# The short sequences' delta rule, moved from behind the prompt's head pairs to between their steps

## The reference

```python
q = _l2norm(q) * dk ** -0.5; k = _l2norm(k)
gc = jnp.cumsum(g, axis=-1)
decay = where(incl, exp(gc[..., :, None] - gc[..., None, :]), 0)
m = where(strict, einsum('bhnid,bhnjd->bhnij', kb, k) * decay, 0)
u, w = triangular_solve(eye + m, [v * beta, kb * exp(gc)])
# per chunk:
v_new = u_n - w_n @ s
o_n = qd_n @ s + qk_n @ v_new
s = s * gt_n + kd_n.T @ v_new
```

## Time and profile before

| what | value |
|---|---|
| median of the runs | 3092.52 us |
| the profiled execution itself | 3093.57 us |
| span of its instructions | 3091.7 us |
| PE busy | 2939.6 us (95%) |
| DVE / ACT / POOL busy | 45% / 29% / 9% |
| DMA | 225.42 MB, mean 73 GB/s |
| mean granted clock of TensorE | 0.947 |

### The profile page before, as it was taken

The page is one execution under the profiler, slowest core; times in us unless marked ns, Lnnn a source line. Parts: engine busy times, 40 slices in busy tenths (PEclk is TensorE's granted clock), DMA queues, the critical chain, the costliest instruction groups (busy, mean ns, idle before and its releaser), DMA issues.

```text
span 3091.7 us, 50936 instructions
## 1 busy us (share of the span) xinstructions
PE 2939.6 (95%) x21018; PEld 2804.5 (91%) x21018; DVE 1378.2 (45%) x1701; ACT 895.8 (29%) x1253; POOL 275.2 (9%) x307
## 2 busy tenths in 40 slices
PE   7999999998898889999999999999999999999997
PEld 6999999987887589999999999999967789999997
DVE  4434357735643354343464443434543434333355
ACT  3222234433221132221233232222344423222232
POOL 4000012202230230000010000000100000000011
PEclk9999999998897589999999999999988889999998
DMA  4222222220002213222222332322211212222221
GB/s 117 76 81 82 82 82 82 82 67 1 3 2 57 68 41 88 87 83 82 72 78 80 127 85 81 87 85 72 94 57 65 81 55 82 82 82 82 78 85 44
DMA packets 306823, 225.42 MB, mean 73 GB/s; under 512 B 8014, under 2 KB 300287, under 8 KB 306687
## 3 DMA queue, kind: packets, MB, share of 16 engines
q1 hardware_dynamic: 306674, 224.30, 24.1%
q0 software_dynamic: 64, 0.00, 0.0%
HBM read 212.14 MB, written 12.13 MB: 73 GB/s over the span
## 4 chain that ended last, share of the span: by engine, by line
PE 91%; DVE 4%; issue 1%; ACT 1%; POOL 1%; DMA 1%; another core or an unknown queue 0%; DVEq 0%; SPq 0%; POOLq 0%; ACTq 0%
PE ps L448 73%; PE ps L1005 2%; PE ps L1018 1%; PE ps L1472 1%; PE ps L1512 1%; PE ps L1015 1%; PE ps L1514 1%; PE ps L1451 1%; PE ps L1479 1%; PE ps L1085 1%; PE ps L1519 1%; PE ps L1097 1%; PE ps L1060 1%; PE ps L1441 1%; DVE w_lo L424 1%
## 5 line engine op out<-in xcount | busy, mean ns | idle before, releaser
L448 PE MATMUL ps<-hx_hi,w_hi 128*128 128x320 f32 (+1 forms) x3986 | 860.7, 297 | 13.0 <-DVE hx_lo L1585 8.5
L448 PE MATMUL ps<-hx_lo,w_hi 128*128 128x320 f32 (+1 forms) x3986 | 860.5, 296 | 0.0
L448 PE MATMUL ps<-hx_hi,w_lo 128*128 128x320 f32 (+1 forms) x3986 | 846.1, 293 | 0.0
L414 ACT ACTIVATE w_hi<-raw 128x1024 fp32r<-128x1024 f32 (+2 forms) x378 | 382.0, 1012 | 1317.4 <-PE ps L448 1300.2
L448 PEld LDWEIGHTS ps<-hx_hi,w_hi 128*128 128x128 f32 x3986 | 606.1, 188 | 15.7 <-issue 7.0
L448 PEld LDWEIGHTS ps<-hx_lo,w_hi 128*128 128x128 f32 x3986 | 617.2, 190 | 0.0
L448 PEld LDWEIGHTS ps<-hx_hi,w_lo 128*128 128x128 f32 x3986 | 610.3, 188 | 0.0
L424 DVE TENSOR_TENSOR w_lo<-raw,w_hi 128x1024 fp32r<-128x1024 f32 (+2 forms) x378 | 470.4, 1245 | 120.8 <-ACT w_hi L414 120.5
L448 PE MATMUL ps<-hid_hi,w_hi 128*128 128x320 f32 (+1 forms) x1664 | 358.5, 297 | 11.1 <-DVE of L910 8.3
L448 PE MATMUL ps<-hid_lo,w_hi 128*128 128x320 f32 (+1 forms) x1664 | 357.4, 296 | 0.0
L448 PE MATMUL ps<-hid_hi,w_lo 128*128 128x320 f32 (+1 forms) x1664 | 356.2, 295 | 0.0
(11 more groups left out here) (364 smaller groups left out, 2558.7 us busy)
## 6 DMA issues: line engine op xcount, KB each, us to landing
raw<-in_ffn_w_in SPq DMA_DIRECT2D x176, 512.0 KB, 5.0
raw<-in_ffn_w_out SPq DMA_DIRECT2D x64, 512.0 KB, 4.3
raw<-in_a_w_in SPq DMA_DIRECT2D x33, 512.0 KB, 4.1
raw<-in_ffn_w_out SPq DMA_DIRECT2D x32, 384.0 KB, 3.4
raw<-in_ple_w_gate SPq DMA_DIRECT2D x16, 512.0 KB, 4.1
raw<-in_w_kv SPq DMA_DIRECT2D x16, 512.0 KB, 4.0
k_page<-in_cache_k SPq DMA_DIRECT2D x16, 512.0 KB, 4.1
v_page<-in_cache_v SPq DMA_DIRECT2D x16, 512.0 KB, 4.4
```

The source lines that it names most:

```text
L414: nc.scalar.activation(w_hi[:, m, 0:k], s.view(m, slot), ACT.Copy).then_inc(w_hi_done, 1)
L448: last = nc.tensor.matmul(TILE[m][:, c0:c1], w[:, m, k], h[:, k, c0:c1], start=k == 0 and a == 0, stop=k == k_all - 1 and a == 2)
```

## The change

- The loop over the pairs is written out four times (`for hp in range(NG)`), so that other steps can stand between those of one pair.
- A lane has three banks instead of four (`lane_bank(a, j)` is bank `3 * a + j`). Banks 6 and 7 belong to the sample steps (`S_BANK`). With a bank less, the broadcast of beta into a lane comes after `qn` has read bank 0, and the transposes of `v` come after `mt` has read bank 1, for both lanes, behind the products.
- The sample steps stand between those of the pairs. In the table (pair, level) is in the inverse, between `am` and `dm` on PE; (pair, i2) is behind chunk 2 of the recurrence.

| pair 0 | pair 1 | pair 2 | pair 3 |
|---|---|---|---|
| level 2 `bc` of q, k | level 1 `am1` | set-up `su4` | set-up `su2` |
| level 3 `bc` of g, beta | level 2 `dm1`, `dtm1` | level 2 read 1 | level 2 `su6` |
| level 4 `kk`, `qk` | level 3 `am2` | level 3 `vtr1` | level 3 read 3 |
| level 5 `vt` | level 4 `dtm2` | level 4 `om1` | level 4 `vtr3` |
| level 6 `kt` | level 5 `wm`, `ut` | level 5 `su1` | level 5 `om3` |
| i2 `xtr` | level 6 read 0 | level 6 `su5` | level 6 `su3` |
| | i0 `vtr0`, i1 `om0`, i3 `su0` | i0 read 2, i1 `vtr2`, i2 `om2` | i0 `su7`, i1 to i3 sums of squares |

- The read, the new rows and the output are made for two heads at a time (q and q + 4, "group q"). DVE, ACT and POOL have their sample steps behind both lanes of a level in the same way, so that what DVE makes in one level PE takes in the next.
- The states of group q are loaded when pair q has used its keys and values, whose place they take.
- The sample tensors move to the place of `w_hi`, `w_lo` and `raw`. The `ab` product therefore prepares no unit of `a_w_out`; `gdn_sp` loads its two first units behind `su7`, and ACT and DVE split unit 0 behind the squares.
- The squares of heads 0 to 5 are made on POOL, those of 6 and 7 on ACT; the sums for heads 0 to 5 stand in the recurrence of pair 3.
- PE takes the row that it spreads from `e32_r`, made once, instead of `sel`, which POOL made for each pair.

```diff
-        following = {id(s): f for s, f in zip(products, products[1:] + [None])}
+        following = {id(s): None if s.kind == "ab" else f for s, f in zip(products, products[1:] + [None])}
@@ the places of the sample tensors
-        r = Region(scratch0, hx1)
-        vnm = [r.at]
+        r = Region(split0, split1)
+        S_BANK = (6, 7)
+        def lane_bank(a, j):
+            return bank(3 * a + j)
+        SUMS = ps[:, 6:8, 0:HC]
@@ gdn_pe
-            with pe.Fori(0, HA // 2) as hp:
+            for hp in range(NG):
...
+                for a in range(2):
+                    h = 2 * hp + a
+                    pe.wait_ge(g["qn"], h + 1)
+                    pick = e32_r[64:64 + HA, h:h + 1].to_broadcast((HA, P))
+                    mm(lane_bank(a, 0), pick, rows_hi[64:64 + HA], start=True, stop=False)
+                    mm(lane_bank(a, 0), pick, rows_lo[64:64 + HA], start=False, stop=True).then_inc(g["bcb"], 1)
+                if hp == 2:
+                    sample_update(0, 4)
+                if hp == 3:
+                    sample_update(2, 2)
...
+                    if (hp, level) == (0, 2):
+                        sample_norms()
...
+            def sample_norms():
+                after(pe, "mq_s", "mk_s", "mg_s", "mb_s")
+                spread(bank_a, dx_s, 0, 2 * HA)
+                done("bcqk_s", spread(bank_b, mt_s, 0, 2 * HA))
+            def sample_read(q):
+                after(pe, "wn_s", "qd_s")
+                if q:
+                    after(pe, f"upd{q - 1 + NG}_s")
+                pe.wait_ge(sample_states_in[q], 64)
+                sw = bank_a[:, 0:2 * NB * 2 * TD].rearrange("p (x t) -> p x t", t=2 * TD)
+                for x, h in enumerate((q, q + NG)):
+                    for b in range(NB):
+                        last = mm(sw[:, x * NB + b], st1(h, b), wq_s[:, h * NB + b], start=True, stop=True)
+                done(f"sw{q}_s", last)
+            def sample_update(q, h):
+                after(pe, f"vnm{h}_s", f"osum{q}_s" if h < NG else f"upd{q}_s")
+                for half in range(2):
+                    last = mm(bank(S_BANK[half]), kd_s[:, h],
+                              vnm[sample_state(q, h) % 2][:, half * PT:(half + 1) * PT].rearrange("p b d -> p (b d)"), start=True, stop=True)
+                done(f"su{h}_s", last)
@@ gdn_dve
+                    if (hp, level) == (0, 1):
+                        sample_spread()
...
+                    if (hp, level) == (2, 5):
+                        sample_update(1)
+                        sample_by_sequence(1, 5)
...
+                    if (hp, i) == (1, 3):
+                        sample_update(0)
+                        sample_by_sequence(0, 4)
...
+            for m in range(2):
+                split_lo(dve, (plan[plan.index(s) + 1], 0, 0), m)
@@ gdn_act
+            for h in range(HA - 2, HA):
+                act.wait_ge(g["osum"], h - 1)
+                nc.scalar.activation(osq[:, h % 2], qkv[:, h], ACT.Square).then_inc(g["osq_last"], 1)
+            for m in range(2):
+                split_hi(act, (plan[plan.index(s) + 1], 0, 0), m)
@@ gdn_pool
+            for h in range(HA - 2):
...
+                if h >= 2:
+                    pool.wait_ge(g["osum"], h - 1)
+                nc.gpsimd.tensor_tensor(osq[:, h % 2], qkv[:, h], qkv[:, h], ALU.mult).then_inc(g["osq"], 1)
```

## The result

The changed kernel takes 3067.82 us (median of five runs, 3064.83 to 3072.09), the kernel before 3092.52. The ratio is 0.9923, 95% interval 0.9911 to 0.9935: faster, by 0.8%. One of the five executions of the kernel before that ran beside it took 4605.10 us, a slow one, which the ratio leaves out. The profiled execution took 3065.89 us, with a span of 3064.2.

A forecast was written before the change was run, and what follows sets the result against it. PE, busy 95% of the span, was taken as the bound. From 3093.57 us: -131.3 + 24.1 + 43.4 + 10.5 + 2.6 + 9.8 + 4.0 + 14 - 2.4 = -25.3, so 3068.3, median 3067 us; 8-in-10 range 3045 to 3085.

The forecast's parts named there:

- Removed and new end: From pair 3's last inverse to the root: 131.3 us of recurrence, short sequences and squares replaced by a 24.1 us end.
- Ahead of the stage: In front of the conv rows: DVE no longer subtracts two half units and ACT's rounding goes, -2.4 us.
- Pairs: Head pairs with sample steps in them: pair 0 some 78 us, pair 1 near 84, pair 2 near 89.
- The set-up with three banks: Each pair's set-up: products start later, waiting for lane 1's `qn` and broadcasts; 1.7 us a pair, 6.8 in all.
- the rival that makes the set-up the bound: Set-ups: PE and DVE stop overlapping with three banks, 40 us instead of 6.8; 3100 us, no change; chance 0.04.
- Updates in the set-ups: Set-ups of pairs 2 and 3: an update at clock 0.53 takes 3.5 us instead of 1.74, 1.5 more each.
- DVE beside POOL: Levels: `vnm` slowed where POOL's masks run; four of eight on the path at 1.0 us each, 4.0.
- New waits: Levels: PE waits for DVE's sample steps (and one ACT exponential), 10.5 us in all, bounds 5 and 14.
- Clock: Levels: at seven places sample steps pull TensorE's clock down, 2.0 us each, 14 in all, ends 0 and 28.
- The rival without a loss of clock: Levels: sample steps do not lower the clock, so the 14 us go: 3053 us; chance 0.26.
- Work of the sample steps: PE's own time for sample steps at full clock, all taken as path: 43.4 us, `su7` counted elsewhere.
- the recurrences: Recurrences of the pairs: DVE's and ACT's sample steps and the `su0` wait at pair 1's end, 2.6 us.

The follow-up runs named there:

- e1: Changed kernel with its three banks a lane, but all sample steps issued in sequence behind the fourth head pair, in banks 6 and 7: 3127.78 us, ratio 1.0125.
- e5: Changed kernel with DVE's four spread tensors of the samples' first step made before the loop over the pairs: 3064.80 us, ratio 0.9911.
- e7: Changed kernel with 112 of the 128 products of the reads of the samples' states left out: 3047.60 us, ratio 0.9854.
- e11: Changed kernel with early spread tensors, values by sequence and masked products first on DVE, TensorE's set-up by lanes, and reads 64 columns wide: 3050.44 us, ratio 0.9865.
- e3: Changed kernel with the updates of heads 4 and 2 moved from the set-ups of pairs 2 and 3 into level 1 of those pairs: 3070.38 us, ratio 0.9931.
- e9: Changed kernel with each read product taking up to 64 columns instead of 16, the excess overwritten by later products: 3061.64 us, ratio 0.9894.
- e8: Changed kernel with each of the 128 products of the reads issued twice in a row into the same place: 3096.23 us, ratio 1.0007.
- e12: e11 with the updates of heads 4 and 2 moved out of the set-ups into level 1, as in e3: 3054.51 us, ratio 0.9881.
- e2: Changed kernel with TensorE's set-up of a pair going lane by lane instead of both beta rows first: 3066.54 us, ratio 0.9925.
- e6: e5 plus two orders on DVE: values by sequence before the update's state is added, masked products before decayed query and decay columns: 3058.75 us, ratio 0.9885.
- e4: Changed kernel with the 32 narrow read products issued eight behind each of lane 1's four dense products, for groups 0, 1 and 3: 3078.91 us, ratio 0.9962.

## Why the prediction was right

3067 us were forecast, 3067.82 measured. The mechanism was the one described: PE's own time for the steps, the waits and the clock took up most of what the sequence gave back. That the number is right to 1 us is luck. The sum for the profiled execution was a gain of 25.3 us; the stage alone gave 32.1, 4.4 were lost behind it, where the sum had nothing, and the median lies 1.9 us above that execution, where it lay 1.05 below before. Term by term:

- *Removed and new end.* 131.3 and 24.1 us; measured 131.2 and 24.0. Inside the 24, POOL's squares took 1.15 us and not the 1.6 that I took from the earlier trace rows, and had slack anyway.
- *Ahead of the stage.* -2.4 forecast, -5.3 measured at the first broadcast. The profile was 1.4 ahead already at its first norm. In e1, e5, e7 and e11, whose first norm comes as in the kernel before, the first broadcast comes 3.0 to 3.9 earlier, so the term is a little larger than forecast.
- *Pairs.* +84.3 forecast (all terms from the sample steps to the clock), +80.4 measured. Pair 0 alone came out 5.6 us over its 78: the waits there were 3.7 and 2.1 instead of 1.9 and 1.2, and the clock fell behind the second too, at 765 us, for 3.4.
- *The set-up with three banks*, 6.8 of the 9.8, is the step that failed. I followed DVE's and PE's lists to the point where `kk` is late and charged the delay. It is there, 5.1 us in e1, but I did not follow it into the levels, where e1 gives back 4.1. In the rival that makes the set-up the bound, the 0.21 us a pass is not what the earlier trace rows show either: 2.08 us for 8 are 0.26, and its time would be some 3110, not 3100.
- *Updates in the set-ups*, 1.74 and 1.5 each: e3 recovered 3.7 and 2.9 for the two. The set-ups of pairs 2 and 3 are longer than e1's by 5.3 and 3.7 us, though, so 2.4 us stood there that were not in the sum.
- *DVE beside POOL*, 4.0: all eight `vnm` together are 0.8 us above 1.21 each. Five had no work of POOL beside them. Of the three that had, one began before POOL's mask and was not slowed, but the mask was, 2.20 us where the median of all 56 is 1.27; one began while a mask ran and took 1.55; one began while a square ran and took 1.73. The first two in the timeline, 922.5 to 924.5 and 985 to 988 us:

```profile
922.93 1.21 DVE L956 TENSOR_TENSOR vnm<-kbg_s,same 64x1024 f32<-64x1024 f32 x1
923.06 2.20 POOL L673 TENSOR_TENSOR dx<-mt,lm 128x512 f32<-128x512 f32 x1 [1.79 <-PE ps L1297]
985.94 1.55 DVE L956 TENSOR_TENSOR vnm<-kbg_s,same 64x1024 f32<-64x1024 f32 x1
```

So the collision was real, and the term was too large because I took the 2.45 of the earlier trace rows as the price and four such meetings on the path.
- *New waits*, 10.5: the sample lines of the list of waits make 3.7, 3.5, 2.1, 1.1 and some of less than 1. Some 12 in all, with the largest where they were forecast.
- *Clock*, 14, and 3 for the updates in the set-ups: outside the set-ups and the first level behind each 27.3 us of low time, half of it 13.7. Six falls, where seven were counted, and not all at the places named: `wm` with `ut` and read 3 have none, and that of 765 us stands behind PE's wait for the masked queries, which had a price as a wait alone. It is in the eight interleaved kernels with the old order of the masked products and in none of the four with the new one. Over all the pairs, set-ups too, (80.4 - 46.2) / 2 = 17.1. The rival without a loss of clock, which had 0.26, is refuted by e7 and e9.
- *Work of the sample steps*, 43.4: the column without clock grew by 63.4 us. Less 12 for waits, 2.6 forecast for the recurrences, 0.8 for `vnm` and the 0.9 by which e1 stands above before, 47 are left, within what that column can tell. Some 2.7 of the 3.7 too many are the halving: at full clock a read took 3.71, not 3.43, and an update 1.98, not 1.74. e7 and e8 give the reads' part alone: at 0.100 and 0.106 a product, 12.8 and 13.6 for the 13.7 of the sum.

What the prediction did not have is the stretch behind the stage. The changed kernel leaves it 32.1 us ahead and ends 27.7 ahead. The windows from the sixth to the seventh of the layers' norms (DVE's reciprocals `rs`), in the kernel before (372.0 us), the changed one (376.6) and e11 (373.6), with all engines:

```profile
2200.40:2572.40 372.00, 359.54 (x2130) 291.96 (x2130) 146.58 (x242) 134.06 (x230) 16.09 (x15) 0.88 0.21 68
```

```profile
2170.10:2546.70 376.60, 364.06 (x2129) 293.50 (x2128) 146.58 (x241) 134.10 (x230) 16.15 (x15) 0.86 0.19 68
```

```profile
2154.50:2528.10 373.60, 361.02 (x2131) 291.76 (x2130) 146.60 (x242) 134.10 (x230) 16.14 (x15) 0.87 0.20 68
```

The work of DVE, ACT and POOL is equal to 0.1 us; PE is busy longer at a lower clock. Low times are 92.3, 102.3 and 95.6 us: 10 us more of it make the 4.6. The same code, reached at another moment, gets another share of full clock. In the twelve experiments the same stage lasted 376.6 to 377.3 us nine times and 373.5 to 374.4 three times (e7, e11, e12). What picks the value is open.

The same holds in small for e2 and e3 against the changed kernel: a fall of the clock in pair 3 came or did not come with the same instructions in the same levels. It can't be said from one profile each whether the edits caused that or whether two executions of one kernel differ so. That runs of e6 reach from 3054.10 us (mean clock 0.960) to 3064.93 (0.957) speaks for a large part of the second.

## What to carry to other kernels

Before you charge a delay in a set-up, follow it through the steps behind it: here 5.1 us of delay stood there, and the levels gave back 4.1, most of it through the clock. Low clock costs half its time where TensorE is packed, and little where it waits anyway, so count it apart for the two. An interleaved step costs its time on the engine that bounds the loop, plus what its kind does to the clock of the work behind it, and that second price is read from rows where the same kind of step runs packed, busy share or not. Where a narrow product lasts as long as a wider one, the wider can be free, and here it left the clock up.

Two parts of one edit can have opposite signs: here banks in sequence cost 33 us and interleaving returned 60. Undo one at a time before you call either good. When you leave work out to price it, count in the trace what is really gone. And where the clock moves a single pair by a few microseconds, a gain of 2 or 3 us in a set-up is not real until the end of the stage shows it.

## What the runs showed of the hardware

- A read of 32 products of up to 64 columns takes 3.64 to 3.72 us, one of 32 products of 16 columns at full clock 3.64 to 3.72 too, 0.116 each. The prompt's products of 128 columns take 1.79 for 16, 0.112 each. What sets their pace was not tested; it is not the columns.
- TensorE, busy for 5.00 of 5.00 us, stands at 0.51 of the clock behind narrow products. Behind the same number up to four times as wide it stands at 1.00, busy for 4.50 of 5.00 us and for 7.00 of 7.00. Eight narrow products behind each dense one (e4) did not hold the clock either.
- DVE's `vnm`, which has two inputs in SBUF, and an instruction of POOL met three times in the changed kernel. The one that began first took its usual time (`vnm` 1.21 us, a mask 1.27, a square 1.14), the other longer (a mask 2.20, `vnm` 1.55 and 1.73).
- The time of a stage that the edit did not touch moved by up to 5 us, all of it clock.
